# Reordering the opening of a fused attention kernel: x in four transfers, high products first, products of zeros ahead of them

## The reference

```python
h = rms_norm(x, norm_gain[layer])
proj = h @ w_in[layer]                       # 1024 x 8448
qa, ka, va, qb, kb, vb, ga, gb, mg = jnp.split(proj, split_idx, axis=-1)
qa = head_rms_norm(qa.reshape(bsz, S, A_Q_HEADS, HEAD_DIM), q_norm_a[layer]) * scale
...
logits = jnp.where(valid, scores + bias, NEG_INF)   # bias looked up by relative position
```

## Time and profile before

| | |
|---|---|
| median of 3 executions | 1232.04 us (1231.27 to 1234.48) |
| profiled execution | 1232.79 us, span in the profile 1230.9 us |
| PE busy | 1175.8 us (96%), granted clock 0.987 in the mean |
| DVE, ACT, POOL busy | 852.6, 548.9, 35.4 us |
| DMA | 207.14 MB, 168 GB/s in the mean |

### The profile page before, as it was taken

The page is one execution under the profiler, slowest core; times in us unless marked ns, Lnnn a source line. Parts: engine busy times, 40 slices in busy tenths (PEclk is TensorE's granted clock), DMA queues, the critical chain, the costliest instruction groups (busy, mean ns, idle before and its releaser), DMA issues.

```text
span 1230.9 us, 17204 instructions
## 1 busy us (share of the span) xinstructions
PE 1175.8 (96%) x6879; PEld 1012.7 (82%) x6879; DVE 852.6 (69%) x1329; ACT 548.9 (45%) x689; POOL 35.4 (3%) x44
## 2 busy tenths in 40 slices
PE   6999999999998798999999999998898999999996
PEld 5888778887996676887999888996676878999885
DVE  4665465656698898787767544698889687776442
ACT  5655555633534453453534433434543543443331
POOL 0232000000000000000000000000000000000000
PEclk9999999999999999999999999999899999999998
DMA  9656554356554232354554655454223444555640
GB/s 308 210 182 235 184 171 146 125 184 214 181 164 167 103 138 103 137 180 165 183 192 171 222 181 201 156 196 165 104 103 108 167 171 171 175 192 181 213 146 35
DMA packets 39615, 207.14 MB, mean 168 GB/s; under 512 B 4119, under 2 KB 13847, under 8 KB 16423
## 3 DMA queue, kind: packets, MB, share of 16 engines
q1 hardware_dynamic: 39104, 204.62, 48.0%
q0 software_dynamic: 96, 1.20, 0.4%
q10 hardware_dynamic: 336, 0.22, 0.1%
HBM read 204.83 MB, written 1.20 MB: 167 GB/s over the span
## 4 chain that ended last, share of the span: by engine, by line
PE 74%; DVE 15%; DVEq 4%; issue 3%; ACT 3%; POOL 0%; DMA 0%; POOLq 0%; ACTq 0%
PE panel L887 16%; PE panel L889 16%; PE panel L888 16%; PE panel L910 6%; PE panel L909 6%; PE panel L908 6%; DVE area L2036 4%; DVE ring_parts L580 4%; PE tile L937 4%; DVEq L2037 2%; PE heads_out L1098 1%; ACT ring_parts L555 1%; DVEq L2106 1%; DVE area L2104 1%; PE panel L925 1%
## 5 line engine op out<-in xcount | busy, mean ns | idle before, releaser
L580 DVE TENSOR_TENSOR ring_parts<-ring,ring_parts 128x2048 fp32r<-128x2048 f32 (+1 forms) x185 | 415.4, 2257 | 163.8 <-ACT ring_parts L555 151.6
L555 ACT ACTIVATE ring_parts<-ring 128x2048 fp32r<-128x2048 f32 (+1 forms) x185 | 348.7, 1888 | 254.8 <-PE panel L889 197.8
L887 PE MATMUL panel<-ring_parts,hT_high 128*128 128x512 f32 (+2 forms) x688 | 281.6, 409 | 15.9 <-DVE ring_parts L580 12.2
L889 PE MATMUL panel<-ring_parts,hT_low 128*128 128x512 f32 (+2 forms) x688 | 267.3, 388 | 0.0
L888 PE MATMUL panel<-ring_parts,hT_high 128*128 128x512 f32 (+2 forms) x688 | 266.4, 387 | 0.0
L908 PE MATMUL panel<-hT_high,ring_parts 128*128 128x256 f32 x704 | 199.4, 283 | 0.0
L910 PE MATMUL panel<-hT_high,ring_parts 128*128 128x256 f32 x704 | 199.2, 283 | 0.0
L909 PE MATMUL panel<-hT_low,ring_parts 128*128 128x256 f32 x704 | 199.2, 283 | 0.0
L887 PEld LDWEIGHTS panel<-ring_parts,hT_high 128*128 128x128 f32 x688 | 130.8, 190 | 49.4 <-issue 23.2
L889 PEld LDWEIGHTS panel<-ring_parts,hT_low 128*128 128x128 f32 x688 | 130.7, 190 | 27.3
L887 PE MATMUL panel<-ring_parts,area_parts 128*128 128x512 f32 x384 | 150.6, 392 | 0.0
(11 more groups left out here) (233 smaller groups left out, 1083.5 us busy)
## 6 DMA issues: line engine op xcount, KB each, us to landing
ring<-in_w_layers_dram SPq DMA_DIRECT2D x140, 1024.0 KB, 4.9
ring<-in_w_first_dram SPq DMA_DIRECT2D x40, 1024.0 KB, 5.0
area<-bias_rows SPq DMA_DIRECT2D x16, 160.0 KB, 3.2
ring<-in_w_layers_dram SPq DMA_DIRECT2D x4, 560.0 KB, 3.8
area<-bias_rows SPq DMA_DIRECT2D x16, 96.0 KB, 3.0
area<-bias_rows SPq DMA_DIRECT2D x1, 1536.0 KB, 8.7
area<-in_gains_dram SPq DMA_DIRECT2D x3, 512.0 KB, 5.8
area_parts<-in_onehot_dram POOLq DMA_DIRECT2D x1, 1170.0 KB, 14.4
```

The source lines that it names most:

```text
L555: act.activation(ring_lo[:, SLOTS + hi, 0:w], ring[:, slot, 0:w], ACT.Copy).then_inc(high_ready, 1)
L580: g.tensor_tensor(ring_lo[:, slot, 0:w], ring[:, slot, 0:w], ring_lo[:, SLOTS + hi, 0:w], ALU.subtract).then_inc(low_ready, 1)
L887: pe.matmul(ps[:, b, 0:width], high, hi[:, k, :], start=first, stop=False)
L889: mm = pe.matmul(ps[:, b, 0:width], low, hi[:, k, :], start=False, stop=last)
```

## The change

- x comes in four transfers: columns 0 to 511 of both blocks ahead of ring half qa/0, columns 512 to 1023 of both behind it. The first gains move from ACT's queue to the head of SP's; the small bias tables move from SP's to ACT's queue.
- ACT runs one tiny activation early. The first piece of qa/0 is rounded by DVE, not by ACT.
- PE multiplies zeros (four products of 128x128 by 128x256 float32, and six more behind the turn of the first columns of x).
- Panel qa is computed by a function of its own: for each half high x high for all k, then x low x weight high, then x high x weight low. The second columns of x are turned inside it.
- `onehot` is loaded when qa/0 has landed, not qa/1. The bias products move: two are in kava (k = 6, 7), seven in qb0. The turn of the heads of qa moves from k = 3 to k = 5 of qb0.

```diff
-BIAS_AT = {("qa", KC - 1): 0, **{("kava", k): k + 1 for k in range(KC)}}
-FIRST_TILES = (by_columns("x") + [f"bias{i}" for i in range(9)]
+BIAS_AT = {("kava", 6): 0, ("kava", 7): 1, **{("qb0", k): k + 2 for k in range(5)}, ("qb0", 6): 7, ("qb0", 7): 8}
+FIRST_TILES = (by_columns("x") + [f"bias{i}" for i in range(7)] + transposed("qa") + ["bias7", "bias8"]
...
             if part.l is None and n == 0:
-                act.activation(ring_lo[:, SLOTS + hi, 0:w // 2], ring[:, slot, 0:w // 2], ACT.Copy).then_inc(first_high, 1)
                 act.activation(ring_lo[:, SLOTS + hi, w // 2:w], ring[:, slot, w // 2:w], ACT.Copy).then_inc(high_ready, 1)
...
-            sp.dma_start(x[:, 0, :], sorted_x[0]).then_inc(x_loaded[0], 16)
-            sp.dma_start(x[:, 1, :], sorted_x[1]).then_inc(x_loaded[1], 16)
+            def load_x(i):
+                for b in range(NB):
+                    cs = slice(i * 512, (i + 1) * 512)
+                    sp.dma_start(x[:, b, cs], sorted_x[b][:, :, cs]).then_inc(x_loaded[i][b], 16)
+            sp.dma_start(first[:, :], a["first"]).then_inc(first_loaded, 16)
+            load_x(0)
...
-            for i in range(3):
-                load_first(i)
-            for copy in range(2):
-                ...
-            for i in range(3, SLOTS):
+            load_first(0)
+            load_x(1)
+            for i in range(1, SLOTS):
                 load_first(i)
...
+            def keep_clock(n):
+                for _ in range(n):
+                    pe.matmul(tile[TILES - 1][:, 0:TOKENS], tok[:, 0, 0:P], tok[:, 0, 0:TOKENS], start=True, stop=True)
+            pe.wait_ge(pad_ready, PADS)
+            keep_clock(4)
+            pe.wait_ge(ident_loaded, 16)
+            def turn_x(i):
+                for b in range(NB):
+                    pe.wait_ge(x_loaded[i][b], 16)
+                    turn(part, f"x{b}{i}", lambda c: x[:, b, (4 * i + c) * P:(4 * i + c + 1) * P])
+            def first_panel():
+                ps, done = panel_for(part, "qa")
...
+                for i in range(2):
+                    ks = range(4 * i, 4 * i + 4)
...
+                    pe.wait_ge(x_high, 2 * i + NB)
+                    if i == 0:
+                        pe.wait_ge(first_high, 1)
+                    else:
+                        pe.wait_ge(high_ready, 2)
+                    for k in ks:
+                        if k == 2:
+                            pe.wait_ge(high_ready, 1)
+                        product(k, hT_hi, high, first=k == 0)
+                    if i == 0:
+                        turn_x(1)
+                    columns_ready(part, "x", i)
+                    for k in ks:
+                        product(k, hT_lo, high)
...
+                    for k in ks:
+                        if k == 2:
+                            pe.wait_ge(low_ready, 1)
+                        mm = product(k, hT_hi, low, last=k == KC - 1)
+                    mm.then_inc(half_used if i == 0 else done, 1)
+            turn_x(0)
+            keep_clock(6)
...
-            act.dma_start(first[:, :], a["first"]).then_inc(loaded, 16)
-            act.wait_ge(loaded, 16 * 2)
+            for copy in range(2):
+                tabs = one("tabs")[BUCKETS * copy:BUCKETS * (copy + 1), :]
+                act.dma_start(tabs[:, 0:32], a["rel_bias"]).then_inc(table_loaded, 16)
+                act.dma_start(tabs[:, 32:40], a["rel_table"]).then_inc(table_loaded, 16)
+            act.wait_ge(pad_ready, PADS)
+            act.activation(brs[:, 0, 0:1], zero, ACT.Identity)
+            act.wait_ge(first_loaded, 16)
...
+            v.memset(tok[:, 0, 0:TOKENS], 0.0).then_inc(pad_ready, 1)
...
-            for b in range(NB):
-                first_low_tile(0, b)
+            first_low_tile(0, 0)
+            name, slot, before, hi = places(part, 0)
+            v.wait_ge(half_loaded[slot], 16)
+            v.tensor_copy(ring_lo[:, SLOTS + hi, 0:HALF // 2], ring[:, slot, 0:HALF // 2])
+            v.drain().then_inc(first_high, 1)
+            first_low_tile(0, 1)
             low_half(v, part, 0)
...
-            g.wait_ge(half_loaded[1], 16)
+            g.wait_ge(half_loaded[0], 16)
             g.dma_start(parts(AREA_1["onehot"], 0, ROW)[0:2 * BUCKETS + 1, :], a["onehot"]).then_inc(onehot_loaded, 16)
```

More of the change, by code:

```diff
@@ L414, in block_kernel @@
         rope_loaded = sem("rotation_loaded")
-        x_loaded = [sem(f"x{b}_loaded") for b in range(NB)]
+        x_loaded = [[sem(f"columns{i}_of_x{b}_loaded") for b in range(NB)] for i in range(2)]
         x_again = sem("x_in_natural_order_loaded")
@@ L882, in rows_out @@
                         first, last = i == 0 and k == 0, i == len(halves) - 1 and k == 3
-                        if half == "qa/0" and k == 2:
-                            pe.wait_ge(low_ready, 1)
                         for b in range(NB):
@@ new lines, in _, with product @@
+            pe.wait_ge(pad_ready, PADS)
+            keep_clock(4)
+            pe.wait_ge(ident_loaded, 16)
+            def turn_x(i):
+                for b in range(NB):
+                    pe.wait_ge(x_loaded[i][b], 16)
+                    turn(part, f"x{b}{i}", lambda c: x[:, b, (4 * i + c) * P:(4 * i + c + 1) * P])
+            def first_panel():
+                ps, done = panel_for(part, "qa")
+                def product(k, of, w, first=False, last=False):
+                    for b in range(NB):
+                        mm = pe.matmul(ps[:, b, :], of[:, k, b * P:(b + 1) * P], w[:, k % 4, :], start=first, stop=last)
+                    return mm
+                for i in range(2):
+                    ks = range(4 * i, 4 * i + 4)
+                    low, high = (ring_lo[:, s, :].rearrange("p (k n) -> p k n", k=4)
+                                 for s in (part.turn("half", f"qa/{i}")[0], SLOTS + part.turn("high", f"qa/{i}")[0]))
+                    pe.wait_ge(x_high, 2 * i + NB)
+                    if i == 0:
+                        pe.wait_ge(first_high, 1)
[11 more added lines that the diff above has]
+                    if i == 0:
+                        pe.wait_ge(first_low, 1)
+                    else:
+                        pe.wait_ge(low_ready, 2)
+                    for k in ks:
[3 more added lines that the diff above has]
+                    mm.then_inc(half_used if i == 0 else done, 1)
@@ L1007, in _ @@
                 if p == "qb0":
-                    between[3] = lambda: turn_heads(0)
-                rows_out(part, p, of_h, two_halves(p), 256 if p == "kava" else 512,
-                         ready=(lambda i: columns_ready(part, "x", i)) if p == "qa" else None, after=between)
+                    between[5] = lambda: turn_heads(0)
+                if p == "qa":
+                    first_panel()
+                else:
+                    rows_out(part, p, of_h, two_halves(p), 256 if p == "kava" else 512, after=between)
                 if 2 <= n <= len(NORMED):
@@ L1368, in _ @@
             for b in range(NB):
-                act.wait_ge(x_loaded[b], 16)
+                for i in range(2):
+                    act.wait_ge(x_loaded[i][b], 16)
                 row_squares(b, b)
@@ L1460, in _ @@
                     if s == 4:
-                        if p == "qb0":
-                            evict_heads(0)
                         round_after(act, part, f"{p}/0")
+                    elif s == 6 and p == "qb0":
+                        evict_heads(0)
                     if (p, s) in BIAS_AT:
@@ L1692, in _ @@
             v.memset(half_power, -0.5).then_inc(pad_ready, 1)
[L1693 removed]
+            v.wait_ge(first_loaded, 16)
+            v.wait_ge(ident_loaded, 16)
             for c in (8, 10):
```

18 lines of the change are left out of this document (5 added, 13 removed).

## The result

The changed kernel takes 1237.28 us (median of 20 executions, 1233.83 to 1238.58); the kernel before, timed beside it, 1233.35 (20 executions, 1230.70 to 1235.62). The ratio is 1.0032, 95% interval 1.0024 to 1.0039: slower by 3.9 us, where 1228.6 was forecast with a range up to 1232.0.

The account below looks back on a forecast made before the run. PE, busy 96%, was taken as the bound, with the row factor behind `onehot` setting qb0's start. qb0 5.1 us earlier less 1.7 for bias products gives 3.4: profiled 1232.79 to 1229.4, median 1228.6, range 1226.0 to 1232.0.

Parts of the forecast that it names:

- PE starts qb0 at R + 5.6: Opening: qb0 waits for its low part, ready 5.6 us after the row factor; start at 30.4, not 35.49.
- qa/0 at 8.6: First ring half of panel qa: lands at 8.6 us (8.2 to 9.0) instead of 9.46.
- The copy 0.9 us: DVE's copy of 1024 columns, rounding the first piece of qa/0: 0.9 us, between 0.6 and 1.22.
- First product 9.6: PE's first product on panel qa: starts at 9.6 us instead of 12.37.
- Clock kept by the zeros: Ahead of panel qa: products of zeros keep PE's clock, saving 1.5 us in qa, hidden while the row factor decides.
- `onehot` 14.4 to land and the drain waits for it: Row factor chain: the transfer takes 14.4 us as before, landing at 23.4, and POOL's drain waits for it.
- R = 24.6: Row factor ready on POOL at 24.6 us instead of 27.79, 3.2 earlier through the earlier issue of `onehot`.
- Waits of 1.3 before kava/1 and 1.0 before qb0, released by DVE: PE's two stops in the opening: about 1.3 us before kava/1, about 1.0 before qb0, both ended by DVE.
- Seven bias products cost 1.7: In qb0, where none was before: seven products of 0.24 us give 1.7 us back.
- A: Row factor chain: `onehot` lands about 3.2 us earlier and the factor decides; 1228.6 (1227.5 to 1229.8), chance 0.48.
- C: DMA engines bound: `onehot` issued earlier but ends as late, factor at 27.8; 1231.6, chance 0.27 including everything towards A.
- D: Shared DMA engines delay qb0/0 to up to 32.8; qb0 starts 1.6 later; slower, 1235.3, chance 0.08.

Follow-up runs that it names:

- a1: The changed kernel once more, nothing altered, for a second profile: 1236.33 us, ratio 1.0033 to the kernel before.
- f4: The changed kernel once more, nothing altered, as a third copy: 1236.20 us.
- f2: The changed kernel with ten more drains on DVE at its start, where it waits for its first loads: 1236.68 us, ratio 1.0029 to the kernel before.
- e3: The changed kernel with 10 discarded products ahead of kava and 14 ahead of qb0: 1235.34 us, ratio 1.0022 to the kernel before.
- g2: The changed kernel with 14 discarded products ahead of qb0 alone: 1236.08 us, ratio 1.0021 to the kernel before.
- e4: The changed kernel with x in two transfers of whole rows, both ahead of qa/0: ratio 1.0035 to the kernel before.
- e5: The changed kernel with `onehot` loaded behind qa/1 again instead of qa/0: 1238.72 us, ratio 1.0038 to the kernel before.
- e6: The changed kernel without its ten products of zeros: 1236.69 us, ratio 1.0030 to the kernel before.
- e7: The changed kernel with POOL's drain in the root of the row factor replaced by a semaphore: 1238.26 us, ratio 1.0041 to the kernel before.
- e9: The changed kernel with `onehot` behind qa/1 and semaphores for the drains in POOL's first two roots: 1232.98 us, ratio 1.0002 to the kernel before.
- e2: The changed kernel with eight of the nine bias products in kava and one in qb0: 1234.29 us, ratio 1.0009 to the kernel before.
- e8: The kernel before with `onehot` loaded behind qa/0 and a semaphore for the drain in the row factor's root: 1231.80 us, ratio 0.9989.
- f3: The kernel before with `onehot` behind qa/0, eight bias products in kava and semaphores for drains in POOL's first two roots: 1232.45 us, ratio 1.0002.

## Why the prediction was wrong

The step that failed is "PE starts qb0 at R + 5.6" (30.2, and 0.2 added for a late half). It looked at one of the two things that qb0 needs, the low part of its first half, and not at its panel buffer, which is that of qa and comes free when DVE has normed qa's heads. By the rows after, from R = 25.92: DVE's sum to 28.46, POOL's factor to 31.93, DVE's read to 33.45, PE 0.1 later: R + 7.6. In the kernel before that chain and PE's own ended within 0.3 us of one another (35.22 and 35.49 in its profile), so nothing waited there and no row named it. The prediction saw that PE started qb0 at R + 7.7 there and put the 2.2 us down to PE's own chain. Eight more profiles (a1, f4, f2, e3, g2, e4, e5, e6) have R from 25.8 to 29.2 and qb0 7.5 to 7.6 behind it. e7 (R 3.2 earlier, head factor late, qb0 later) and e9 (head factor early, qb0 at 30.85) show that the link is the head factor. 2.0 us went here. Another 1.3 went by R itself, 25.92 instead of 24.6.

A second thing was missing from the prediction: ACT squares the heads of qa behind its rounding of kava/1. `onehot`, issued early, holds that half back: it lands at 24.8, and at 17.5 with `onehot` late (e5). In the changed kernel ACT is free at 25.95 and R comes at 25.92, a tie again, so that bringing R forward alone (e7) gains nothing, and bringing both forward (e9) does.

Point by point:

- *qa/0 at 8.6*: 10.2. With four transfers of half rows the queue moves 0.59 MB instead of 1.24 in 3 us; e4 restores it. `onehot`, which waits for this half, was 1.3 late with it. The bounds (8.2 to 9.0) were too narrow: they were made with the rate of the earlier trace rows, which whole rows had given.
- *The copy 0.9 us*: 0.69, near the lower bound. The Trainium skill ("VectorE: DVE Perf Modes", "The perf-mode tier table") gives a float32 copy twice the rate of a subtraction of two tensors; the trace agrees, 0.69 against 1.21 for 1024 columns.
- *First product 9.6*: 11.04. *Clock kept by the zeros*: in the first profile yes, in a copy no. Both are free in e6, as said.
- *`onehot` 14.4 to land and the drain waits for it*: 14.2, and e7 shows the drain. *R = 24.6*: 25.92, by the late landing.
- *Waits of 1.3 before kava/1 and 1.0 before qb0, released by DVE*: 1.64 and 1.99, both by DVE, and neither the one that was meant. The first is ahead of kava/0, which landed at 22.7 (22.8 in f4, but 15.8 in a1) where it was 13.4 before, and has nothing to do with R; the second is for the read of qa.
- *Seven bias products cost 1.7*: 1.65 by their starts, 0.24 each, but 2.0 from qb0's start to M by the table. They lie behind the gate on qb0, where they cost in full; e2 has six of them ahead of it.
- *Rivals*: R did come between A and C, but none had qb0 late by the head factor. D had the right sign, and its mechanism was at work on the wrong half: qb0/0 landed at 27.3, 3.0 later than before and past the 27 that was named as a sign of being wrong, but D needed 29.5; it was kava/0 and kava/1, 9 us later than before, that PE and ACT waited for.
- *The clock*: the prediction gave its falls 1.7 us "either way". A fall behind qb0 is one way only: no wait stands behind it that could hide it, and the kernel before has none there in any of its profiles.
- *Slips that change nothing in the sum*: "POOL waited until 11.79" takes the length of an idle time for a moment (it began at 0.43, and `onehot` was issued at 12.22); the middle of 7.2 and 12.5 is 9.9 and not 9.6; high qa/1 by its own terms comes at 16.6 and not 16.3, 0.3 more of a room of 2.1.

The sum by measured terms, for the two profiled executions: qb0 earlier by 35.49 - 33.56 = 1.93, the seven bias products +2.0, the fall +1.5, together +1.6, as at M. From the forecast, 3.4 the other way, it is 5.0 away: 1.3 by R, 2.0 by the path behind it less the 0.2 that was added, 0.3 by the bias products, 1.5 by the fall. Up to M that account closes within 0.1. The 0.8 in the layers is put down to DVE's gaps; against the copy of the kernel before, whose layers took 2.9 us more with 2.7 us of gaps, it can't be shown.

For the typical execution it closes less well. Put together, 126 executions of the kernel before, timed beside the experiments, have a mean granted clock of 0.9887 and a mean time of 1233.1; 28 of the changed kernel and its copies have 0.9874 and 1236.8. 90 of the 126 have 0.989 or more, 4 of the 28. The difference, 0.0013 of 1232, is 1.6 us of full clock missing, what one fall takes; with 0.8 for DVE's gaps that is an estimate of 2.4 of 3.7. It is a rough one, as a fall ahead of a wait lowers the mean clock and costs nothing: of the two first profiles the changed kernel's has the higher clock and the longer span. The last 1.3 us are open: no profile caught an execution of the changed kernel above 1236.2 us. A longer fall in the opening, as e4 and e7 have behind longer waits, would give it; that is argued, not shown. That the clock falls there because of the waits is supported by all 20 profiles, and no run had the same opening with and without the waits alone.

## What to carry to other kernels

A gate has several inputs, and where two chains end within a few tenths of each other the trace names at most one: before shortening one, list everything that the gated work needs, its output buffer too, and date each. Work moved from a place where the engine waits to one where it doesn't costs in full, though it is the same work. A transfer that is brought forward pushes others back: look for who waits for those. And where two profiles of one program differ by more than the gain (578.1 and 581.0 us for the layers here), take a second profile of the kernel before, before you explain what happens far from the change: a marker that moves 2.6 us forward (e9) may leave the median of many executions where it was.

## What had not been expected of the hardware

- With x in 512-column rows (2 KB), two transfers ahead of qa/0 and two behind it, the hardware queue moved 0.20 MB/us instead of 0.41 (0.59 and 1.24 MB in 3 us; 0.57, 0.63, 0.67 and 0.88 in a1, f4, e6 and e5); with rows of 4 KB, both ahead, it was 0.42 (1.27 MB in e4, which has the four tiny transfers of the bias tables too). Which of the two, the short rows or the place in the queue, does it was not separated.
- A software transfer of 1.17 MB, issued 4.5 us earlier (10.45 and 14.92), held a half of 0.5 MB on the hardware queue back by 7.3 us (kava/1, 24.8 against 17.5 in e5).
- A drain on POOL waits for POOL's own DMA: the power starts 0.09 us after its input with a semaphore, 4.73 with the drain (e7; in e8, e9 and f3 too it starts with `onehot` still under way).
- The same power on 128x16 took 2.92 us in 19 profiles and 5.07 in e7. The cause is open.
- DVE has gaps of 0.4 us with no releaser at places that move with the number of instructions ahead of them (3.1 us in the layers before, 2.7 in its copy, 4.2 with six drains more). What makes them is open.
